# Two transformer blocks in one kernel: where block 2's differential norm and first output operands stand, and in which PSUM banks the output product begins

## The reference

```python
for l in range(2):
    h = rms_norm(x, norm_g[l])
    proj = h @ w_in[l]            # (256, 6726): a_q a_k a_v a_f a_gate b_cq b_ckv b_krope b_gate c_q c_k c_v c_gate
    a_out = fox_attention(...) * silu(a_gate)          # 6 heads of 128
    b_out = mla_attention(...) * silu(b_gate)          # 6 heads of 128
    c_out = diff_attention(...)                        # 4 heads of 128
    c_out = rms_norm(c_out, diff_subln_g[l]) * (1 - lam_init)   # mean of squares over each head's 128 columns
    c_out = c_out * silu(c_gate)
    x = x + concat(a_out, b_out, c_out) @ w_out[l]     # (256, 2048) @ (2048, 2048)
return rms_norm(x, final_norm_g)
```

## Time and profile before

| | us |
|---|---|
| three executions | 2133.17, 2131.01, 2130.09 |
| median | 2131.01 |
| span of the profiled execution (first to last instruction) | 2133.0 |
| PE busy in it | 2060.0 (97%) |
| DVE busy | 1404.8 (66%) |
| ACT busy | 1007.5 (47%) |
| POOL busy | 130.0 (6%) |
| DMA, mean over the span | 217 GB/s |

### The profile page before, as it was taken

The page is one execution under the profiler, slowest core; times in us unless marked ns, Lnnn a source line. Parts: engine busy times, 40 slices in busy tenths (PEclk is TensorE's granted clock), DMA queues, the critical chain, the costliest instruction groups (busy, mean ns, idle before and its releaser), DMA issues.

```text
span 2133.0 us, 33911 instructions
## 1 busy us (share of the span) xinstructions
PE 2060.0 (97%) x13976; PEld 1865.6 (87%) x13976; DVE 1404.8 (66%) x2153; ACT 1007.5 (47%) x1490; POOL 130.0 (6%) x113
## 2 busy tenths in 40 slices
PE   5999999998999999999999999999999999999997
PEld 1679998787999999998888899999978999999876
DVE  2358999886667677666566676456566656565565
ACT  2234445534454454444545465344555545445454
POOL 0000000022000000000011011000001110000100
PEclk6999999999999999999999999999999999999999
DMA  9998798684777777656655546545545556545553
GB/s 362 383 359 308 239 393 324 216 312 148 232 236 235 227 242 262 190 157 244 192 178 199 178 153 198 200 142 161 176 158 182 171 161 205 172 158 171 166 178 119
DMA packets 267317, 462.97 MB, mean 217 GB/s; under 512 B 21526, under 2 KB 160028, under 8 KB 266652
## 3 DMA queue, kind: packets, MB, share of 16 engines
q1 hardware_dynamic: 265832, 459.66, 63.9%
q10 hardware_dynamic: 1332, 1.14, 0.2%
HBM read 458.62 MB, written 2.13 MB: 216 GB/s over the span
## 4 chain that ended last, share of the span: by engine, by line
PE 84%; DVE 7%; DMA 3%; ACT 2%; issue 2%; ACTq 1%; POOL 0%; SPq 0%; DVEq 0%
PE PS L312 36%; PE PS L311 20%; PE PS L1359 7%; PE PS L1364 7%; PE PS L1360 7%; DVE WLO L302 2%; PE PS L1202 2%; ACT WHI L294 1%; DMA BIG<-w_ada 1%; PE PS L413 1%; DMA X<-x 1%; PE PS L1216 1%; DVE WK L1041 1%; DVE BIG L1687 1%; PE PS L1031 0%
## 5 line engine op out<-in xcount | busy, mean ns | idle before, releaser
L302 DVE TENSOR_TENSOR WLO<-RAWT,WHI 128x1024 fp32r<-128x1024 f32 (+7 forms) x694 | 830.3, 1203 | 405.6 <-ACT WHI L294 404.7
L294 ACT ACTIVATE WHI<-RAWT 128x1024 fp32r<-128x1024 f32 (+7 forms) x694 | 694.0, 1015 | 358.4 <-PE PS L1364 198.9
L312 PE MATMUL PS<-WHI,HH 128*128 128x512 f32 (+5 forms) x1304 | 507.3, 389 | 17.9 <-DVE HLO L789 7.3
L312 PE MATMUL PS<-WHI,HLO 128*128 128x512 f32 (+5 forms) x1304 | 497.8, 382 | 0.0
L312 PE MATMUL PS<-WLO,HH 128*128 128x512 f32 (+5 forms) x1304 | 340.7, 383 | 0.8 <-DVE WLO L302 0.8
L1359 PE MATMUL PS<-HH,WHI 128*128 128x256 f32 x1376 | 328.6, 280 | 7.1 <-POOL HLO L1050 7.1
L1360 PE MATMUL PS<-HLO,WHI 128*128 128x256 f32 x1376 | 327.3, 279 | 0.0
L311 PE MATMUL PS<-HH,WHI 128*128 128x256 f32 x1280 | 311.8, 285 | 0.0
L312 PEld LDWEIGHTS PS<-WHI,HH 128*128 128x128 f32 x1304 | 246.2, 189 | 66.7 <-DVE HLO L789 14.6
L311 PE MATMUL PS<-HLO,WHI 128*128 128x256 f32 x1280 | 303.1, 278 | 0.0
L312 PEld LDWEIGHTS PS<-WLO,HH 128*128 128x128 f32 x1304 | 245.6, 189 | 43.2 <-DVE WLO L302 1.6
(11 more groups left out here) (301 smaller groups left out, 1614.0 us busy)
## 6 DMA issues: line engine op xcount, KB each, us to landing
RAWT<-w_in SPq DMA_DIRECT2D x96, 1024.0 KB, 5.2
RAWT<-w_up SPq DMA_DIRECT2D x168, 512.0 KB, 4.9
AD<-w_ada SPq DMA_DIRECT2D x152, 512.0 KB, 6.3
RAWT<-w_out SPq DMA_DIRECT2D x96, 512.0 KB, 4.9
RAWT<-w_down SPq DMA_DIRECT2D x86, 512.0 KB, 4.6
BIG<-w_ada SPq DMA_DIRECT2D x40, 512.0 KB, 12.2
RAWT<-w_in SPq DMA_DIRECT2D x16, 832.0 KB, 4.5
RAWT<-w_in SPq DMA_DIRECT2D x16, 512.0 KB, 4.6
```

The lines of the kernel that those rows point to most:

```text
L294: act.activation(WHI[:, (q % HL) * GR:(q % HL) * GR + size], r, ACT.Copy).then_inc(S("hi_done"), 1)
L302: dve.tensor_tensor(WLO[:, (q % HL) * GR:(q % HL) * GR + size], r, h.bitcast(F32), ALU.subtract)\
L312: pe.matmul(o, feat, weight, start=start, stop=stop)
```

## The change

**What it does.** Four things, in both layers of block 2:

- `out2_start` is new and stands between `block2_input` and `kout` for ACT and DVE. ACT's eight sums of squares, DVE's eleven small steps, the feature splits of groups 0 and 1, ACT's weight splits of groups 0, 1 and 2 and DVE's of groups 0 and 1 move into it.
- The Silu eviction of the last gate piece, which was ACT's first step after the input product, is now the last step of ACT's `out2_start`.
- `diff_norm` is cut in two: `diff_stats` (above) and `diff_scale` (DVE's four large multiplications), which keeps its place after DVE's group 2.
- PE's first group of the output product is `first_half`: six matmuls into banks 2 and 3, then a wait for the last gate piece's eviction, then six into banks 0 and 1. The number of matmuls is the same, and in each bank the three terms follow each other.

SP and POOL keep their instructions and their order.

```diff
--- before.py
+++ after.py
@@ -746,11 +746,42 @@
                     if t >= 112:
                         for fn in beside[t]:
                             fn()
+
+        def out2_start(eng, who, l, tally, chain=None):
+
+
+            g0 = place[f"w_out_2{l}"][0]
+            st0 = tally.at("st")
+
+            def split(i):
+                if who == "act":
+                    if i == 0:
+                        eng.wait_ge(S("gated2"), 2 * l + 1)
+                    eng.wait_ge(S("mm_done"), 2 * g0 - 2)
+                    eng.activation(HHv[:, 8 + i, :], merged2(i), ACT.Copy).then_inc(S("st_hi"), 1)
+                else:
+                    eng.wait_ge(S("st_hi"), st0 + i + 1)
+                    eng.tensor_tensor(HLv[:, 8 + i, :], merged2(i), HHv[:, 8 + i, :].bitcast(F32), ALU.subtract)\
+                       .then_inc(S("st_lo"), 1)
+
             if who == "act":
+                hi(eng, g0, 0, 4, 0, GR)
+                eng.wait_ge(S("sm_o_out"), outputs(tally.at("sm")))
+                diff_stats(eng, who, l, tally)
+                split(0)
+                hi(eng, g0, 0, 4, 1, GR)
+                split(1)
+                hi(eng, g0 + 1, 0, 4, 0, GR)
                 piece_out(eng, who, pieces[l][-1])
+            else:
+                lo(eng, g0, 0, 0, GR)
+                split(0)
+                diff_stats(eng, who, l, tally, chain)
+                split(1)
+                lo(eng, g0, 0, 1, GR)
 
         def kout(eng, who, name, w, kts, src, tally, macs=None, ring=8, wait=None, beside=None, second=None,
-                 early=None, order=None, ahead=()):
+                 early=None, order=None, ahead=(), split_ahead=(), first_banks=None):
 
 
             g0 = place[name][0]
@@ -776,7 +807,7 @@
                     eng.dma_start(raw_slot(gs)[:, j * GR:(j + 1) * GR],
                                   w[kt * P:(kt + 1) * P, c * GR:(c + 1) * GR]).then_inc(raw_in[gs % RAW], 16)
                 elif who == "act":
-                    if split:
+                    if split and i not in split_ahead:
                         if wait:
                             wait(eng, kt)
                         ge(eng, S("mm_done"), max(q - 3, 2 * g0 - 2))
@@ -801,7 +832,9 @@
                         for h in range(2):
                             parts.append((2 * n2 + h, PS[:, 4 * c + 2 * n2 + h, :], HHv[:, r, h * P:(h + 1) * P],
                                           HLv[:, r, h * P:(h + 1) * P], WHI[:, o:o + 512], WLO[:, o:o + 512]))
-                    if c == 1 and n == kts - 2:
+                    if i == 0 and first_banks:
+                        first_half(eng, parts, q, first_banks)
+                    elif c == 1 and n == kts - 2:
                         before_last = parts
                     elif c == 1 and n == kts - 1:
                         last_two(eng, q - 1, (before_last, parts))
@@ -818,10 +851,23 @@
                 if beside and c == 1:
                     beside(eng, kt)
                 if early and c == 0:
-                    if ahead and n == 7:
+                    if order and ahead and n == 7:
                         early(eng, n, {"act": weight_hi, "dve": weight_lo}.get(who))
                     else:
                         early(eng, n)
+
+        def first_half(pe, parts, q, free):
+
+
+            pe.wait_ge(S("hi_done"), q + 1)
+            pe.wait_ge(S("lo_done"), q + 1)
+            for pair in (1, 0):
+                free[pair](pe)
+                for bank, o, lh, ll, wh, wl in parts[2 * pair:2 * pair + 2]:
+                    pe.matmul(o, lh, wh, start=True, stop=False)
+                    pe.matmul(o, ll, wh, start=False, stop=False)
+                    mm = pe.matmul(o, lh, wl, start=False, stop=False)
+            mm.then_inc(S("mm_done"), 1)
 
         def last_two(pe, q, parts):
 
@@ -2137,9 +2183,8 @@
 
 
             def go(e, kt):
-                if who == "act" and kt == 1 or who == "dve" and kt == 2:
-                    e.wait_ge(S("sm_o_out"), outputs(tally.at("sm")))
-                    diff_norm(e, who, l, tally, chain)
+                if who == "dve" and kt == 2:
+                    diff_scale(e, l, chain)
                 for k in range(2):
                     if kt == (4 if who == "pe" else 7) + k:
                         if who == "pe" and k == 0:
@@ -2196,19 +2241,20 @@
                 eng.wait_ge(S("ln_act"), l + 1)
                 eng.wait_ge(S("ln_dve"), l + 1)
 
-        def diff_norm(eng, who, l, tally, chain=None):
+        def diff_stats(eng, who, l, tally, chain=None):
             parts = [(b2(h, CQ + i * P), WK[:, (4 * h + i) * P:(4 * h + i + 1) * P]) for h in range(2) for i in range(4)]
             rms(eng, who, parts, [P] * 8, tally, chain)
-            if who == "dve":
-                for h in range(2):
-                    v = b2(h, CQ, 512).rearrange("p (a x) -> p a x", a=4)
-                    op = eng.tensor_tensor(v, v, ST[:, 24 + 4 * h:28 + 4 * h].unsqueeze(2).broadcast_to((P, 4, P)),
-                                           ALU.mult)
-                chain(op)
-                evicted(eng, pieces[l][-1])
-                for h in range(2):
-                    op = eng.tensor_tensor(b2(h, CQ, 512), b2(h, CQ, 512), b2(h, CG, 512), ALU.mult)
-                op.then_inc(S("dn_out"), 1)
+
+        def diff_scale(dve, l, chain):
+            for h in range(2):
+                v = b2(h, CQ, 512).rearrange("p (a x) -> p a x", a=4)
+                op = dve.tensor_tensor(v, v, ST[:, 24 + 4 * h:28 + 4 * h].unsqueeze(2).broadcast_to((P, 4, P)),
+                                       ALU.mult)
+            chain(op)
+            evicted(dve, pieces[l][-1])
+            for h in range(2):
+                op = dve.tensor_tensor(b2(h, CQ, 512), b2(h, CQ, 512), b2(h, CG, 512), ALU.mult)
+            op.then_inc(S("dn_out"), 1)
 
         WEV1 = prod["w_in"].c0 + 11
         NSET, NLATE = 11, 12
@@ -2334,10 +2380,11 @@
                 block2_input(act, "act", l, first=late_x("act", prep), second=input_norm("act", l, ty, chain),
                              beside=block2_beside(act, "act", l, ty))
                 turned(act, ty)
+                out2_start(act, "act", l, ty)
                 prep = prep_x("act", 1, None, ty)
                 kout(act, "act", f"w_out_2{l}", w_out_2[l], 16, merged2, ty, beside=early_x("act", 1, prep, None) if l == 0
                      else lambda e, kt: rms_x_squares(e, 24, 0, xn_junk) if kt == 8 else None,
-                     early=block2_tail(act, "act", l, ty),
+                     early=block2_tail(act, "act", l, ty), ahead=(0, 1, 2), split_ahead=(0, 1),
                      wait=lambda e, kt, l=l: turned(e, ty) if kt == 12 else
                      e.wait_ge(S("gated2"), 2 * l + 1 + kt // 6) if kt in (0, 6) else None)
             rms_x(act, "act", 24, ty, chain)
@@ -2465,12 +2512,13 @@
             for l in range(2):
                 block2_input(dve, "dve", l, first=late_x("dve", prep, add), second=input_norm("dve", l, ty, chain),
                              beside=block2_beside(dve, "dve", l, ty, chain))
+                out2_start(dve, "dve", l, ty, chain)
                 prep = prep_x("dve", 1, lambda kt: PV[:, V_NG + 16 + kt:V_NG + 17 + kt], ty)
                 first = lambda e, l=l: kout_add(e, "dve", f"w_out_2{l}", 16, 0, ty, False)
                 add = lambda e, l=l: kout_add(e, "dve", f"w_out_2{l}", 16, 1, ty, False)
                 kout(dve, "dve", f"w_out_2{l}", w_out_2[l], 16, merged2, ty, beside=early_x("dve", 1, prep, first) if l == 0
                      else lambda e, kt, first=first: first(e) if kt == 1 else None,
-                     early=block2_tail(dve, "dve", l, ty, chain))
+                     early=block2_tail(dve, "dve", l, ty, chain), ahead=(0, 1), split_ahead=(0, 1))
             add(dve)
             dve.wait_ge(S("x_add"), 32)
             rms_x(dve, "dve", 24, ty, chain)
@@ -2589,7 +2637,8 @@
                 stat = ty.at("ts")
                 prep = prep_x("pe", 1, None, ty)
                 kout(pe, "pe", f"w_out_2{l}", w_out_2[l], 16, None, ty, second=lambda e: turned(e, ty),
-                     beside=early_x("pe", 1, prep, None) if l == 0 else None, early=block2_tail(pe, "pe", l, ty))
+                     beside=early_x("pe", 1, prep, None) if l == 0 else None, early=block2_tail(pe, "pe", l, ty),
+                     first_banks=(lambda e, l=l: evicted(e, pieces[l][-1]), lambda e, l=l: evicted(e, pieces[l][-2])))
 
 
 _NAMES = ["x", "c", "positions", "w_ada", "b_ada", "norm1_g", "w_in", "sb_norm_g", "dsa_norm_g", "w_out", "norm2_g",
```

## The result

| | before | after |
|---|---|---|
| median of 4 executions, us | 2132.09 (2130.09 to 2135.7) | 2119.49 (2119.27 to 2122.05) |
| ratio, with its 95% interval | | 0.9946 [0.9931, 0.9961] |
| span of the profiled execution, us | 2133.0 | 2117.4 |

The forecast was 2119.5 us. The ratio is not the quotient of the two medians, which is 0.9941: they lie 12.6 us apart. Its interval is wide against the forecast: it stands for 8.3 to 14.7 us, so the times alone would not tell a gain of 9 from one of 14. The profile does.

What follows compares the result with a forecast made beforehand. PE was taken to set the pace in block 2, with two waits per layer worth 13.33 us; less 2 x 0.3 gives 12.7. From a median of 2131.0, less 11.1 to 12.7, it forecast 2119.5 us, range 2117 to 2122.

Steps and rivals of the forecast that it cites:

- the term of the clock: PE in layer 1 after the second wait: the clock's fall cost 1.59 us, counted among the 13.33 to be had.
- Two waits with two causes: PE, each layer: 2.70 us before output group 0 from ACT's late splits, about 2.6 before group 3 from DVE's late part.
- The splits are hidden in ACT's idle time: ACT before the gate's eviction: 10.41 us idle holds squares and splits, done 1.8 us before the eviction; cost 0.
- The half slot: PE's first output group: six matmuls, 1.37 us, run beside the gate's eviction, leaving 0.3 us per layer (0.1 to 1.7).
- Group 3 has a lead of 2.1 us: DVE's feature part for output group 3 is ready 2.1 us before PE needs it, so nothing of the second wait remains.
- The sum: Both layers: 13.33 us less 2 x 0.3 gives 12.7 off the profiled span, 11.1 without the clock.
- The forecast's step from span to median: Whole kernel: profiled execution taken as near the slowest run, 2133.17 us, with the median 2131.01 about 2 us lower.
- the second stall: Rival, before group 3: DVE stays late and only the first wait goes; 2124.3 to 2125.9 us, chance 0.07.
- the half slot did hide its work: Its rival, PE's first output group: nothing is hidden beside the eviction, 1.4 us more per layer, 2122.3 us; chance 0.09.
- the change did what it says: Its rival, `out2_start`: a step waits for something after the gate, so nothing improves; 2128 to 2133 us, chance 0.04.
- the load was not late: Its rival, ACT: a late weight load delays the third weight split and the eviction; slower, 2135 us, chance 0.03.

Runs made afterwards that it cites:

- Only norm sums: Kernel before with only ACT's squares and DVE's eleven small steps put ahead of the gate's eviction; 2128.76 us, ratio 0.9960 to before.
- norm sums late: Changed kernel with ACT's squares and DVE's small steps back behind output groups 1 and 2; 2123.91 us, ratio 0.9946 to before.
- small steps late: Changed kernel with only DVE's eleven small steps back behind group 2, ACT's squares still early; 2120.18 us, ratio 0.9930 to before.
- before again: Kernel before, unchanged, in a second profiled execution; 2135.44 us in one run.
- no half slot: Changed kernel, but PE's output group 0 waits for the whole gate eviction before it starts; 2121.11 us, ratio 0.9937 to before.
- eviction later: Changed kernel with a fourth weight split ahead of the gate's eviction on ACT; 2122.34 us in one run.

## Why the prediction was right, point by point

The waits, their causes and what hides the moved work held in every step of the sum; the term of the clock was no fixed amount, and the last digits of the time were luck.

- **Two waits with two causes.** Right. "Only norm sums" takes away the second and leaves the first; "norm sums late" the other way round.
- **The splits are hidden in ACT's idle time.** Right. Forecast: the third weight split done 1.8 us before the eviction; measured 1.62. The eviction kept its time to 0.01 us.
- **The half slot.** Forecast 0.3 us of excess per layer; measured 16.81 less 16.47, 0.34: 0.24 of wait and 0.08 of restart are 0.32 of it.
- **Group 3 has a lead of 2.1 us.** Measured 2.3, and used up to the tenth by "small steps late".
- **The sum.** 12.7 forecast on the profiled execution, 12.64 measured in the two stretches and 12.5 by the span less the mark. (The forecast puts the second wait "two groups later"; by the rows it is three, groups 0, 1 and 2. No term hangs on it.)
- **The clock.** The term of 1.6 us was right for that profile, but it is no fixed term. The fall follows such waits irregularly, in either layer, costs nothing when a later wait covers it, and 1.5 to 2.9 us when none does. In the stretches of four profiled executions there were 11 waits of 2.1 us or more and 6 falls behind them (before: 1 of 4, before again: 2 of 3, norm sums late: 1 of 2, only norm sums: 2 of 2). Behind the shorter ones (1.66 twice in no half slot, 1.02 twice in eviction later, the 1.01, and the gaps of 0.24 in both layers of after, small steps late and norm sums late) there was none in eleven. What decides between a fall and none was not found. The Trainium skill (TensorE: Matmul & The Clock Gate, Part 1) says that idleness halves the clock and that the chip's observation is not tied to the kernel's own time, so that the moment of a change varies from run to run. The trace agrees as far as it goes: in layer 0 the same waits of 2.70 and 2.6 us were followed by a fall in one execution and not in the other.
- **How the profile stands to the times.** One step was wrong: I took the profiled execution for the one of 2133.17. In the profiles since then the time is 1.8 to 2.1 us above the span (2119.28 for 2117.4, 2135.44 for 2133.5), so the profile of before belongs to about 2134.9, nearest to the fourth execution's 2135.7 and 2.8 above the median. The forecast's step from span to median, "about 2 us", came from the wrong pair. Two misses cancelled: from the median to the forecast I took off 11.5 us, where the medians lie 12.6 apart, and the fourth execution lifted the median before from 2131.01 to 2132.09. The value 2119.5 therefore met the median to 0.01 us by luck; with single runs 3 us apart after and 11 apart before, anything from 2118 to 2122 would have been as good an answer.

The rivals: the second stall did not stay, the half slot did hide its work, the change did what it says, and the load was not late (the third weight split waited 0.86 us for PE, not for a load, in the rows above).

## What to carry to other kernels

When an engine waits at a seam between two products, look at the other engines' orders: here ACT stood idle for 10 us ahead of an instruction that could not start, with others behind it that could. Write the work that needs nothing of the seam ahead of the wait, and begin the new product in the banks that are already free. Follow the second wait back as well; it had a cause of its own, and of the two moves that looked alike (squares on ACT, small steps on DVE) only the first one gave time, 2.4 us per layer at full clock. And set a short stretch around the change beside the times: with 3 to 13 us between the fastest and the slowest run of a kernel, the variants that differ by 0.3 to 3 us are told apart only there.

## What the runs showed of the hardware

- After waits of PE of 2.1 to 2.7 us the granted clock fell to half for some us in 6 of 11 cases; the same kernel showed both. The price of such a wait was its length and up to 2.9 us more.
- ACT's eviction of two banks took 1.27 us beside PE's writes to two others, as long as alone (1.27 in the kernel before, 1.26 in no half slot).
- In no half slot two fulfilled waits stood behind the blocking one, and 0.36 us lay between the releaser's end and PE's start instead of 0.15. That they are the cause was not shown.
